# Moving one block's attention, Fourier mixing and transposes from the third block's expert gather into the second's

## The reference, cut to what matters

```python
for l in range(DEPTH):
    mix, (ka, va, kb, vb) = token_mix_context(yp * (1 + sc1) + sh1, ...)
    yp = layer_norm(ALPHA * yp + g1 * mix, ln1_g[l], ln1_b[l])
    yp = layer_norm(ALPHA * yp + g2 * peer_ffn(yp * (1 + sc2) + sh2, *ffn), ln2_g[l], ln2_b[l])
    ...
    mix = token_mix_latent(ys * (1 + sc1) + sh1, cache_na_k[:, l], ...)
    ys = layer_norm(ALPHA * ys + g1 * mix, ...)
    ys = layer_norm(ALPHA * ys + g2 * peer_ffn(ys * (1 + sc2) + sh2, *ffn), ...)

def one(args):                      # in peer_ffn, for a block of 128 tokens
    a = jnp.einsum('tkd,td->tk', u_tab[e_blk], x_blk)
    w = g_blk * gelu(a)
    return jnp.einsum('tk,tkd->td', w, v_tab[e_blk])
```

## Time and profile before

| | |
|---|---|
| median of three runs | 2348.08 us (2341.66, 2348.08, 2356.87) |
| profiled execution | 2342.3 us, span of its instructions 2340.5 us |
| TensorE matmul busy | 1942.0 us (83%) |
| VectorE busy | 1601.9 us (68%) |
| ScalarE busy | 857.6 us (37%) |
| GpSimd busy | 872.8 us (37%) |
| moved by DMA | 956.73 MB, of them 805.36 MB in the gather's queue |

### The profile page before, as it was taken

How to read it: one execution, slowest core, us unless ns; L and a number is a source line. 1 busy time by engine, 2 the same in 40 slices (tenths; PEclk the granted TensorE clock), 3 DMA queues, 4 the chain that set the end, 5 groups by cost and what they waited for, 6 DMA issues and landing times.

```text
span 2340.5 us, 22659 instructions
## 1 busy us (share of the span) xinstructions
PE 1942.0 (83%) x7010; PEld 1069.0 (46%) x7010; DVE 1601.9 (68%) x3505; ACT 857.6 (37%) x2600; POOL 872.8 (37%) x772
## 2 busy tenths in 40 slices
PE   7999888998879777888968889999787777777776
PEld 5667555764335222344633555666333322322222
DVE  0259988799984445655697788799889845544544
ACT  2344465433333222452333458233333322322222
POOL 0021446323323343343334443534354443443441
PEclk9999999999989999999999999999899999999999
DMA  9989999999999999999999999999999999999996
GB/s 394 420 355 400 422 401 421 418 393 384 421 421 421 421 421 422 390 421 420 419 421 413 421 413 366 419 414 421 421 386 421 421 422 421 422 422 421 422 421 278
DMA packets 139305, 956.73 MB, mean 409 GB/s; under 512 B 15664, under 2 KB 21936, under 8 KB 24624
## 3 DMA queue, kind: packets, MB, share of 16 engines
q0 software_dynamic: 110592, 805.36, 83.2%
q1 hardware_dynamic: 24160, 143.80, 15.0%
q10 hardware_dynamic: 4432, 6.12, 0.8%
HBM read 952.86 MB, written 2.36 MB: 408 GB/s over the span
## 4 chain that ended last, share of the span: by engine, by line
DMA 45%; PE 26%; DVE 20%; issue 4%; ACT 4%; POOL 1%; SPq 0%; ACTq 0%; DVEq 0%; POOLq 0%
DMA uv_rows<-in_peer_uv,experts 43%; PE acc L873 15%; DVE uv_rows L1454 7%; PE pair L898 6%; POOL uv_rows L766 1%; DVE arena L1368 1%; PE pair L908 1%; DVE dve_sum L1440 1%; DMA wtiles<-in_w_mod 1%; PE pair L1000 1%; ACT diag L1102 1%; DMA wtiles<-in_w_in 1%; DVE best_j L1365 1%; DVE best_j L1374 1%; DVE top_i L1365 1%
## 5 line engine op out<-in xcount | busy, mean ns | idle before, releaser
L873 PE MATMUL acc<-uv_rows,diag 128*128 128x512 f32 x2736 | 1281.7, 616 | 285.7 <-ACT diag L1102 277.5
L766 POOL DMA_INDIRECT uv_rows<-in_peer_uv,experts x768 | 872.6, 1136 | 1433.7 <-PE acc L873 1182.1
L1454 DVE CUSTOM_DVE_ANT_0 uv_rows<-uv_rows,h_tok 128x1024 f32<-128x1024 f32 x768 | 934.1, 1225 | 560.3 <-DMA uv_rows<-in_peer_uv,experts 552.7
L873 PEld LDWEIGHTS acc<-uv_rows,diag 128*128 128x128 f32 x2736 | 512.6, 195 | 992.0 <-issue 536.5
L1089 ACT ACTIVATE gelu<-dots 128x2 f32<-128x2 f32 x384 | 78.2, 204 | 1120.7 <-DVE dots L1454 1119.7
L1102 ACT ACTIVATE diag<-consts,weight 128x128 f32<-128x128 f32 x684 | 233.9, 386 | 6.5 <-PE acc L873 6.2
L898 PE MATMUL pair<-wtiles,hT 128*128 128x256 f32 x880 | 198.9, 387 | 15.0 <-ACT arena L1036 9.1
L898 PEld LDWEIGHTS pair<-wtiles,hT 128*128 128x128 f32 x880 | 170.8, 195 | 49.2 <-issue 10.9
L1093 ACT ACTIVATE weight<-gelu,gates 128x1 f32<-128x1 f32 x768 | 184.2, 287 | 12.6
L908 PE MATMUL pair<-hT,wtiles 128*128 128x256 f32 (+1 forms) x896 | 158.1, 334 | 0.0
L908 PEld LDWEIGHTS pair<-hT,wtiles 128*128 128x128 f32 x896 | 140.4, 191 | 15.7 <-issue 3.3
(11 more groups left out here) (123 smaller groups left out, 1251.6 us busy)
## 6 DMA issues: line engine op xcount, KB each, us to landing
wtiles<-in_w_mod SPq DMA_DIRECT2D x28, 1024.0 KB, 10.5
wtiles<-in_peer_wq SPq DMA_DIRECT2D x28, 1024.0 KB, 9.4
wtiles<-in_w_in SPq DMA_DIRECT2D x21, 1024.0 KB, 9.7
uv_rows<-in_w_mod SPq DMA_DIRECT2D x20, 1024.0 KB, 18.8
uv_rows<-in_peer_uv,experts POOLq DMA_INDIRECT x768, 17.8
wtiles<-in_w_out SPq DMA_DIRECT2D x12, 1024.0 KB, 9.4
uv_rows<-in_w_in SPq DMA_DIRECT2D x7, 1024.0 KB, 31.0
uv_rows<-in_w_out SPq DMA_DIRECT2D x4, 1024.0 KB, 18.2
```

The source lines that it names most:

```text
L766: pool.indirect_dma_start(out=uv_rows[:, slot, :, :].rearrange("p t d -> p (t d)"), out_offset=None, in_=i["peer_uv"], in_offset=bass.Indi ...
L873: last = nc.tensor.matmul(acc[:, half, :], diag[:, summed_before(n)[0] % DIAGS, :], uv_rows[:, slot, 1, half * 512:(half + 1) * 512], star ...
L1454: nc.vector.tensor_tensor_reduce(out=uv_rows[:, slot, 0, :], in0=uv_rows[:, slot, 0, :], in1=h_tok[:, q % 3, :], scale=1.0, scalar=0.0, op ...
```

## The change

`mix_middle(2)` moves from the gather of block 2 to the gather of block 1, directly behind `mix_start(2)` and ahead of `gate2(1)` and `ln2(1)`. The tables of places are replaced from the end of block 0's gather to the end of block 3's, and a few numbers later on. Two rows fewer are added by VectorE: in block 0 rows 35 and 41 go to TensorE and row 36 comes from it; in block 3 row 50 goes to TensorE.

```diff
-    s += beside(1, woven(route_steps(2), fill) + mix_start(2))
-    s += beside(2, mix_middle(2) + mix_end(2) + query_steps(2))
+    s += beside(1, woven(route_steps(2), fill) + mix_start(2) + mix_middle(2))
+    s += beside(2, mix_end(2) + query_steps(2))
...
 PLACES = {
     "pe": (
...
-        "0 2 0 2 0 0 0 0 0 0 0 2 0 0 0 0 4 0 0 0 0 0 0 0 0 0 0 2 0 4 0 0 6 4 0 2 0 2 0 2 74 0 0 0 0 0 0 16 2 0 6 2 0 8 2 "
+        "0 2 0 2 0 0 0 0 0 0 0 2 0 0 2 0 2 0 0 0 0 0 0 0 1 0 0 0 0 5 0 0 0 0 0 1 0 0 0 1 1 1 2 3 0 1 1 0 0 2 0 0 2 0 1 2 "
...
 SUMMED_BY_DVE = {
-    0: (16, 20, 21, 23, 25, 29, 32, 33, 35, 41, 42, 44, 45, 47, 49, 55, 60, 61, 67, 73, 75, 76, 77, 78, 79, 80, 81, 83,
-       93, 94, 95, 96, 97, 98, 99),
-    3: (1, 3, 4, 5, 6, 7, 8, 9, 10, 12, 13, 14, 16, 17, 18, 19, 21, 24, 27, 29, 33, 39, 41, 42, 43, 44, 50, 53, 54, 55,
-       56, 57, 58, 59, 61, 63, 65, 71, 72, 73, 74, 75, 76, 77, 87, 90, 92, 93, 95),
+    0: (16, 20, 21, 23, 25, 29, 32, 33, 36, 42, 44, 45, 47, 49, 55, 60, 61, 67, 73, 75, 76, 77, 78, 79, 80, 81, 83, 93,
+       94, 95, 96, 97, 98, 99),
+    3: (1, 3, 4, 5, 6, 7, 8, 9, 10, 12, 13, 14, 16, 17, 18, 19, 21, 24, 27, 29, 33, 39, 41, 42, 43, 44, 53, 54, 55, 56,
+       57, 58, 59, 61, 63, 65, 71, 72, 73, 74, 75, 76, 77, 87, 90, 92, 93, 95),
```

## The result

The changed kernel takes 2357.06 us (median of 20 runs, 2351.75 to 2364.58) against 2347.39 us for the kernel before on the same chip: a ratio of **1.0048**, 95% interval 1.0037 to 1.006. It is some 10 us slower where 3 us faster were forecast. Its profiled execution took 2363.26 us, with a span of 2361.5 us. Busy times hardly change (TensorE 1961.3 us, VectorE 1600.6, ScalarE 852.0, GpSimd 864.2), nor do the bytes.

The account below looks back on a forecast made before the run. The DMA engines were taken to bound the kernel (2272.5 of 2340.5 us). Terms -4.3 + 1.5 + 0 + 0 + about 0.3 gave about -3 us, from 2348.1 to 2345 us by medians; range 2334 to 2360 us.

Parts of the forecast that it names:

- rival 1: Block 1's gather, turns 1.040 to 1.051: waits within the dense mixing exceed 7 us of cover; +4.3 us, 2352 us, chance 0.18.
- The release of `acc`: End of block 1's gather: released ahead of turn 2.002 on VectorE, the hole goes; -4.3 us, between -4.3 and 0.
- slice 21: A 58.5 us slice of the rate table with 1.1 us idle, counted with slice 16 as 5.4 us winnable.
- slice 16: Slice with the hole at block 1's end, at 390 GB/s, 4.3 us idle; forecast to rise to 421.
- The start of block 2's gather: Four `outp` tiles together at turn 2.003, 16.4 us of TensorE with one row; price 0, ends 0 and +2 us.
- Rival 2: The hole only moves to turns 2.003 to 2.012 and the 4.3 us come back; 2348 us, chance 0.15.
- The mixing in block 1's gather: Turns 1.036 to 1.052: TensorE falls 10.7 us behind under 17.8 us of cover; +1.5 us, ends 0 and +8.6.
- the share under 0.9: Sign of rival 1: a DMA share below 0.9 between turns 1.036 and 1.056.
- The clock: Rival 3: four waits in the dense mixing, each paying 3.1 us for TensorE's slow clock; +1 us, 2349 us, chance 0.07.
- The other places: Shifted places outside the named steps: slices 8 and 9 at 0, rows that change hands 0 to +1 us.
- slices 8 and 9: End of block 0's gather, 9.0 us idle: query projection two turns earlier on TensorE; 0, ends -2 and +2 us.
- The rows that change hands: Of three rows exchanged between VectorE and TensorE, two net go to TensorE, 1.8 us each; 0 to +1 us.

Follow-up runs that it names:

- Run 3: Changed kernel with mix 2's seven projection tiles spread three rows apart and the mixing behind them 16 turns later: 2352.42 us, ratio 1.0017 to the kernel before.
- run 6: Kernel before with only mix 2's projection tiles, transposed input and norm at the change's bunched places; attention, gate and layer norm stay: 2362.92 us, ratio 1.0087.
- run 2: Kernel before with only the change's places and rows from mix 3's second transpose to the end: 2347.17 us, ratio 1.001.
- run 1: Changed kernel with the old places and rows from mix 3's second transpose to the end: 2350.14 us, ratio 1.0015 to the kernel before.
- the second execution: Changed kernel, unchanged, profiled a second time: span 2352.6 us, first dot at 150.5 us.
- run 9: Kernel before with only the change's places and VectorE rows for block 0's gather: 2349.33 us, ratio 1.002.
- run 4: Changed kernel with mix 2's tiles spread and blocks 0, 3 and later as in the kernel before: 2347.37 us, ratio 1.0003 to the kernel before.
- run 8: As run 4, with mix 2's attention steps about two turns apart and block 1's gate later: 2344.13 us, ratio 1.0004 to the kernel before.

## Why the prediction was wrong

The forecast was 0 to -6 us; measured are +9.7 us. That 2357 us still lies within the range that was given, 2334 to 2360 (2333 to 2361 by its own terms), is luck: its upper end was rival 1 on the highest single run, and no rival of the prediction reaches +9.7. Nor was 1% the least that can be told here: 20 runs of each kernel tell 0.48%.

**The release of `acc`: right.** Forecast -4.3 us. Turns 0 to 15 of block 2 lose 0.2 us in place of 3.1 to 4.3, and the routing's end loses 0.0 in place of 1.3 to 2.3, which the prediction counted among what could be won in slice 21 and left out of the sum. All signs named for it came: a DMA share of 1.01, GpSimd's wait under 12 us, the first row of block 2 5.1 us behind the last of block 1, slice 16 at 421.

**The start of block 2's gather: right.** Price 0; turns 0 to 31 of the kernel after lose 0.5 to 0.6 us. Rival 2 (the hole only moves) fell.

**The mixing in block 1's gather: the step that failed first.** Its sum set 67.9 us of TensorE work against 57.2 us of transfers over the whole of turns 1.036 to 1.052 and found 10.7 us of arrears under 17.8 us of cover. But the seven tiles stand in the first half with three rows between them, the other rows in the second. The same terms, summed over the bunch alone: at 703.8 us, where GpSimd's last issue ended, 6.5 rows were still to be moved (by the packets in the trace). Until its issue at 742.1 us, 38.3 us, the DMA engines had these, four `proj` tiles and the rows issued at 720.77, 731.78 and 736.95, 13.5 x 2.49 = 33.6 us; the three `outp` tiles, which the prediction counted in, stood behind `kvout` until 743.2 us. That gives a hole of 4.7 us, where 4.5 were measured, and 1.9 more were lost until 748 us. Nothing was lost before 731 us; from then on TensorE gave one slot free for each tile and row, every 5.2 us, for a row that takes 2.49 us to move. So this term, forecast at +1.5 us, came to 6.1 to 8.8 us in turns 40 to 55. Rival 1 had the direction and the size (8.6 us), and the share under 0.9 that was to show it came, but it had the wrong cause, waits inside the attention. Run 3 spreads the tiles and the hole goes; run 6 bunches them without the attention and it is there.

**The clock: no cause of its own, but a part of the size.** In the bunch the mean granted clock was 0.84 and 0.96 up to 720 us and 1.00 from there, and the first three tiles took 12.31 us in place of 3 x 3.62 = 10.9. In the second execution they ran at a granted clock of 1.00, in 10.63 us, and turns 40 to 55 lost 6.1 us all the same; in the third one tile more was slow, 5.38 us in place of 3.69, and they lost 8.8. In block 3 the transposes took 3.98 us in place of 1.92 in the first execution alone. In both places TensorE stood still first (3.00 and 2.01 us), though the second execution kept its clock at 1.00 behind the same wait of 2.99 us. The Trainium skill, "TensorE: Matmul & The Clock Gate", Part 1, has the slow clock as the default that activity lifts; the traces agree (0.50 at 708 to 710 us, 1.00 from 712 us on). So the lower clock can lengthen a hole (6.3 and 8.8 us against 6.1 in block 1, 4.8 against 2.4 and 3.4 in block 3), and no run shows one that it made alone.

**The other places: the larger failure.** The prediction took 0 for slices 8 and 9, with ends of 2 us either way, and never compared the tables in block 3's second half, where the change moves mix 3's last attention steps two to four turns later on ScalarE and VectorE and leaves TensorE's. In their place the runs show 4.6 us for block 0's shift (425.4 - 420.8, of them 3.0 us of lost time) and 2 to 8 us for block 3's (run 2: 1.001, 2.1 us lost; after against run 1: 0.0033). The prediction had the rule for it in its own text (how many turns ahead TensorE is asked to wait) and applied it only to the steps that the change is named after.

**The rows that change hands** weren't tried by themselves; they are part of runs 1, 2 and 9.

**What stays open.** Turns 16 to 31 of block 3 lose 1.9 to 3.7 us in every kernel with the attention moved and 0.5 to 1.6 in every one without; the tables are alike there, and the cause wasn't found. It takes back some 2 us of what block 2 gains and may be a part of why runs 4 and 8 measure as no change. By which of its steps block 0's shift works was not tried step by step.

## What to carry to other kernels

When a ring of buffers hides a slow consumer, balance work and transfers over each stretch without a freed slot, not over the whole of a stage: seven tiles nearly in a row cost 6 to 9 us, and the same tiles three turns apart nothing. Read every engine's place of every step that a change touches, above all of those that it isn't named after; a step that waits for another engine five turns ahead in a ring of ten costs 2 to 5 us, one at seven turns 11 us. And profile the same kernel several times before a term of 5 us is put down to an edit.

## What the runs showed of the hardware

Up to the first dot product the program is the same in all kernels, yet that dot came between 146.4 and 155.2 us. The traces part at TensorE's granted clock. Busy time by stretch in the third execution of the kernel before (first dot at 155.2 us):

```profile
60.00:80.00 20.00, 17.70 (x128) 11.81 (x126) 1.35 (x5) 8.02 (x25) 0.00 (x0) 0.84 1.02 419
80.00:100.00 20.00, 19.63 (x179) 13.29 (x179) 4.96 (x19) 9.63 (x40) 0.00 (x0) 0.82 1.01 422
```

and in the third of the changed kernel (147.1 us):

```profile
60.00:80.00 20.00, 16.70 (x153) 10.69 (x151) 3.45 (x13) 10.63 (x38) 0.00 (x0) 0.95 1.02 419
80.00:100.00 20.00, 18.13 (x166) 12.74 (x163) 4.08 (x12) 9.36 (x31) 0.00 (x0) 0.96 1.01 422
```

At the same 419 to 422 GB/s, the mean granted clock is 0.84 and 0.82 in the one and 0.95 and 0.96 in the other. The twenty profiled executions bear it out: five have 0.76 to 0.84 in both stretches, and their first dot comes at 153.9 to 155.2 us; five have 0.94 to 0.97 in both, and it comes at 146.4 to 148.4 us. The other ten have 0.91 to 1.00 there and come between, at 149.2 to 153.0 us, so these two stretches are not the whole of it. That the clock is the cause, and what sets it, was not tried. The start alone differs by up to 8.8 us, nearly as much as the whole change costs.
